# Two more weight-block subtractions per expert made by POOL in a mixture-of-experts kernel

## The reference, cut to what matters

```python
aff = softmax(h @ w_router)                     # 1024 tokens, 16 experts
gates, idx = lax.top_k(aff.swapaxes(1, 2), 128) # each expert takes 128 tokens
xin = h[idx]                                    # gather, 128 x 1024 for each expert
a = xin @ w_gate[e]; b = xin @ w_up[e]          # 1024 x 1024 each
y = (silu(a) * b) @ w_down[e]                   # 1024 x 1024
out[idx] += y * gates                           # scatter with addition
```

## Time and profile before

| | us |
|---|---|
| median of 3 runs | 2973.61 (2973.12 to 2975.37) |
| the profiled execution, its own time | 2971.25 |
| its span in the trace | 2969.4 |
| PE busy | 2826.3 (95%) |
| DVE busy | 1794.0 (60%) |
| ACT busy | 1216.6 (41%) |
| POOL busy | 461.3 (16%) |

### The profile page before, as it was taken

How to read it: one execution, slowest core, us unless ns; L and a number is a source line. 1 busy time by engine, 2 the same in 40 slices (tenths; PEclk the granted TensorE clock), 3 DMA queues, 4 the chain that set the end, 5 groups by cost and what they waited for, 6 DMA issues and landing times.

```text
span 2969.4 us, 35888 instructions
## 1 busy us (share of the span) xinstructions
PE 2826.3 (95%) x14252; PEld 2309.4 (78%) x14252; DVE 1794.0 (60%) x2535; ACT 1216.6 (41%) x1952; POOL 461.3 (16%) x423
## 2 busy tenths in 40 slices
PE   8999999999998999999995999999999999999998
PEld 6876788778885588888874887878878868588888
DVE  3633688430433788888885677877778764110554
ACT  4222677241321477777766124454443342011101
POOL 1400122000001211121104000000000153132231
PEclk9999999999998999999997999999999999999999
DMA  4120000330213999999984121030110221010131
GB/s 137 73 101 22 29 1 1 129 112 29 93 43 126 366 383 396 395 396 391 397 310 142 57 85 57 19 111 26 68 55 23 93 69 60 25 57 29 54 131 57
DMA packets 141459, 382.25 MB, mean 129 GB/s; under 512 B 11744, under 2 KB 45026, under 8 KB 141165
## 3 DMA queue, kind: packets, MB, share of 16 engines
q1 hardware_dynamic: 125036, 324.17, 28.8%
q0 software_dynamic: 13520, 46.28, 4.9%
q10 hardware_dynamic: 2736, 9.50, 0.9%
HBM read 340.47 MB, written 39.46 MB: 128 GB/s over the span
## 4 chain that ended last, share of the span: by engine, by line
PE 87%; DVE 7%; ACT 3%; issue 1%; DMA 1%; POOL 1%; SPq 0%; DVEq 0%; POOLq 0%; ACTq 0%
PE ps L2643 7%; PE ps L2310 7%; PE ps L2644 7%; PE ps L2645 7%; PE ps L2296 6%; PE ps L2628 6%; PE ps L2630 6%; PE ps L2629 6%; PE ps L2702 2%; PE ps L2704 2%; PE ps L2703 2%; PE ps L2745 2%; PE ps L2714 1%; PE ps L2716 1%; PE ps L2715 1%
## 5 line engine op out<-in xcount | busy, mean ns | idle before, releaser
L2072 DVE SCALAR_TENSOR_TENSOR b_f<-b_f,small_f 128x1023 f32<-128x1023 f32 (+14 forms) x240 | 304.3, 1268 | 34.8 <-ACT small_f L1202 17.5
L2643 PE MATMUL ps<-x_f32r,w_f32r 128*128 128x512 f32 x480 | 188.4, 393 | 0.8 <-issue 0.8
L2645 PE MATMUL ps<-x_f32r,w_f32r 128*128 128x512 f32 x480 | 187.2, 390 | 0.0
L2629 PE MATMUL ps<-w_f32r,a_f32r 128*128 128x512 f32 x456 | 177.5, 389 | 0.0
L2644 PE MATMUL ps<-ht_f32r,w_f32r 128*128 128x512 f32 x416 | 162.4, 390 | 0.0
L2703 PE MATMUL ps<-w_f32r,a_f32r 128*128 128x512 f32 x384 | 152.1, 396 | 0.0
L2296 PE MATMUL ps<-small_f 128*128 128x128 f32 (+1 forms) x632 | 89.9, 288 | 50.5 <-DVE small_f L1725 30.2
L2643 PE MATMUL ps<-ht_f32r,w_f32r 128*128 128x512 f32 x320 | 126.8, 396 | 9.4 <-issue 4.8
L2296 PEld LDWEIGHTS ps<-small_f 128*128 128x128 f32 (+1 forms) x632 | 76.4, 145 | 64.0 <-DVE small_f L1725 32.2
L2645 PE MATMUL ps<-ht_f32r,w_f32r 128*128 128x512 f32 x320 | 126.0, 394 | 0.0
L2629 PE MATMUL ps<-x_f32r,a_f32r 128*128 128x512 f32 x312 | 121.9, 391 | 0.0
(11 more groups left out here) (477 smaller groups left out, 7942.7 us busy)
## 6 DMA issues: line engine op xcount, KB each, us to landing
w_f<-in_w_exp_up SPq DMA_DIRECT2D x40, 1024.0 KB, 9.8
w_f<-in_w_exp_down SPq DMA_DIRECT2D x38, 1024.0 KB, 8.1
w_f<-in_w_exp_gate SPq DMA_DIRECT2D x36, 1024.0 KB, 8.1
x_f<-in_w_exp_gate SPq DMA_DIRECT2D x28, 1024.0 KB, 8.3
x_f<-in_w_exp_down SPq DMA_DIRECT2D x26, 1024.0 KB, 8.2
x_f<-in_w_exp_up SPq DMA_DIRECT2D x24, 1024.0 KB, 9.6
w_f<-in_w_in SPq DMA_DIRECT2D x22, 1024.0 KB, 5.1
w_f<-in_w_in SPq DMA_DIRECT2D x10, 2048.0 KB, 7.7
```

Source lines behind the costliest of these rows:

```text
L2072: ins = v.scalar_tensor_tensor(C_conv[k][:, d:S], U_conv[k][:, 0:S - d], cols[:, k, R_TAP + j:R_TAP + j + 1], C_conv[k][:, d:S], ALU.mult, ...
L2629: mm(o, x1, w2[:, k, c], start=False, stop=False)
L2643: mm(o, l1, r1, start=(k == 0), stop=False)
L2645: ins = mm(o, l2, r1, start=False, stop=(k == n - 1))
```

## The change

POOL makes lo for quarter 1 of gate and of up of experts 1 to 15 (30 units, U1 and G1 in the steady state) besides unit 0. DVE makes the other 161. POOL does each in its loop at the place of that unit: U1 lies ahead of the scatter (which stands at U2), and G1 behind the gather (which stands at G0). TensorE waits for these 30 on POOL's semaphore.

```diff
-        LO_POOL = [0]
+        LO_POOL = [0] + [n for n, (m, e, q) in enumerate(UNITS) if e >= 1 and m != "d" and q == 1]
         LO_DVE = [n for n in range(len(UNITS)) if n not in LO_POOL]
...
-            for n in LO_POOL:
-                pool_lo(n)
+            pool_lo(0)
...
             for n in range(len(UNITS) + 3):
+                if n > 0 and n in LO_POOL:
+                    pool_lo(n)
                 for e in range(2, NE):
                     if n == unit["g", e - 1, 0]:
                         gather(e)
```

## The result

The changed kernel takes 2978.98 us (median of 20 runs), the kernel before 2972.51 us (20 runs): ratio 1.0023, 95% interval 1.0016 to 1.0030. It is slower by 6.5 us, where 7.3 us were forecast.

What follows compares the result with a forecast made beforehand. PE was taken as the bound, busy throughout each expert's 34.46 us. Fifteen G1 waits of 0.49 us sum to 7.3 us, added to 2973.6 for a forecast of 2980.9 us; range 2973 to 2994.5.

Steps and rivals of the forecast that it cites:

- PE is the bound; relief for DVE is worth nothing: In one expert's stretch PE is never idle, so taking 4.6 us off DVE's 30.37 gains nothing.
- The engines exclude each other, and POOL's G1 ends a fixed time behind DVE's G0: With two SBUF inputs on DVE, the later operation waits; POOL's G1 ends 4.47 us after DVE's G0.
- The size of the wait: At each G1 PE starts 0.39 us late and loses 0.10 restarting: 0.49 us, ends 0.27 and 0.8.
- The restart: After the wait at G1, PE's first five matmuls take 1.23 us instead of 1.13, another 0.10.
- It repeats 15 times and does not grow: G1 of experts 1 to 15: PE's shift moves the whole chain, the same 0.49 us each, 7.3 us.
- DVE catches up, U1 has slack: After G2's hold DVE stands 0.49 us later, like PE; POOL's U1 ends with 1.7 us slack, no wait.
- POOL not ready: Rival at G1: gather's issue is held by DVE's G0, POOL 0.9 us later on 14 experts; 2994, chance 0.15.
- No wait at all: Rival at G1: POOL starts at hi, ends before PE's need; no or tiny wait, 2973.6 to 2976, chance 0.20.
- DVE the bound: Rival across each expert: mutually exclusive subtractions make DVE's period 37.3 us, 42 us more, 3015; chance 0.05.

Runs made afterwards that it cites:

- the kernel with quarter 2: The change, but POOL makes lo for G2 and U2 instead of G1 and U1 of experts 1 to 15; 2972.26 us, 1.0007 of the kernel before.
- The experiment with 3 us: The change, plus three settings to zero on POOL ahead of each of its G1 subtractions; 2998.37 us, 1.0085 of the kernel before.

## Why the prediction was right, step by step

**PE is the bound; relief for DVE is worth nothing.** Right. With U1 taken off DVE the stage is the same to 0.1 us.

**The engines exclude each other, and POOL's G1 ends a fixed time behind DVE's G0.** Right, and shown by an experiment: with PSUM readers in place of DVE's G0 from SBUF at POOL's start, POOL's 5.64 us become 4.64. The reckoned 4.47 us from DVE's end to POOL's were 4.51 at G1.

**The size of the wait.** Forecast 0.49 us for each G1, measured 0.375. The term that was mis-sized is the way from the input's end to PE's first matmul. I took 0.25 us, from PE behind DVE's line 2014; behind POOL it is 0.05 (1244.48 to 1244.53). So PE is 0.23 us late and not 0.39: 0.04 more through the 4.51, 0.20 less through this way. The restart costs a little more than reckoned: the next five intervals take 1.26 us, 0.13 over 5 x 0.227, for which 0.10 was set. 0.23 + 0.13 = 0.36, close to the 0.375 per expert. With the right figure the sum would have been 15 x 0.375 = 5.6 us, just under the 5.9 us that the prediction took as the least that can be told from no change.

**It repeats 15 times and does not grow.** Right: 15 waits, period 34.81 us (POOL's G1 at 1238.84 and 1273.65; forecast 34.95).

**DVE catches up, U1 has slack.** Right: no wait at U1 in any profile. In the expert shown POOL's U1 ends at 1230.69 and PE starts it at 1232.49, 1.8 us later (forecast 1.7). The forecast durations of line 1078, 5.6 at G1 and 5.4 at U1, were 5.64 and 5.5; those of DVE's G2 and U2, 3.8 and 5.6, were 3.9 (6.14 less 2.20) and 5.9.

**The rivals.** *POOL not ready* did not come: the gather's issue took 1.00 us at 1237.23. It began 0.46 us ahead of DVE's G0 (1237.69), less than the 0.6 to 1.2 reckoned, and was still running when G0 began. In the kernel with quarter 2 it begins 0.10 us behind G0's start and takes 3.04 us, so the margin was real and small. The scatter's did get held up, 3.60 in place of 1.60, as that case had said. The experiment with 3 us shows what this case would have cost. *No wait at all* fell with the 5.64 us. *DVE the bound* did not come: the blocked time lay beside its waits for ACT and PE.

**The rest of the 6.5 us.** The 5.62 us are shown. The difference of the medians leaves 0.9, less than its own uncertainty (the interval 1.0016 to 1.0030 is 4.8 to 8.9 us). The clock in the last down product gave 1.3 to 2.9 us in the profiles of the change; the forecast had no term for it. That the 6.5 us lie as near to the forecast 7.3 as they do, and above the 5.9, is in part luck: the wait gives 5.62, and what adds the rest isn't shown.

## What to carry to other kernels

Before moving an elementwise operation from DVE to POOL, look up whether the operation that will run beside it on DVE reads two inputs from SBUF. Here the moved one then ended its full 4.5 us after that one's end, and DVE, relieved of 68 us of work, stood still for some 80. What a helper engine loses costs nothing until it passes the consumer's need, and then it costs in full each time. So choose by distance to the need (quarter 2 was free, quarter 1 was not), or let the consumer do first what doesn't need the late input. Where the bound engine has no idle time at all, moving work among the others can't gain, and the only question is what it can lose.

## What the runs showed of the hardware that was not expected

- From POOL's end to PE's first matmul it was 0.05 us, in the change and in the kernel with 3 us (1254.36 to 1254.41); behind DVE's line 2014 it was 0.25 us. The runs don't say whether this is the engine, or that the latter wait stands behind transposes.
- The issue of an indirect DMA by POOL is held up by a DVE subtraction with two SBUF inputs that has already begun: the scatter takes 3.60 us in place of 1.60 in 15 of the 16 experts of the change, and the gather 3.04 in place of 1.00 in the kernel with quarter 2. The Trainium skill (SBUF — State Buffer, "Practical consequences") infers that tensor_tensor takes only the read interface and leaves the writing of descriptors alone; these rows don't show which interface is held, but the issue is longer by the rest of DVE's subtraction.
- TensorE's granted clock fell to 0.50 for up to 6 us behind two waits of PE (0.9 and 1.8 us) in some executions, and stayed at 1.00 behind the same waits in others.
